# A decoder layer on one core: the sparse heads' scaling and biases moved to GpSimd, the compressed branch's output matmul split in two f32r parts

## What is computed

```python
kc = compress(k_cmp, ...); vc = compress(v_cmp, ...)      # 31 compressed keys and values of each group
pc = softmax(q . kc - m * dist)                           # compressed branch
o_c = pc @ vc
ps = softmax(q . ks - m * dist)                           # selected blocks (at 512 tokens: all, causal)
pw = softmax(q . kw - m * dist)                           # sliding window of 512
o = gate0 * o_c + gate1 * (ps @ vs) + gate2 * (pw @ vw)
```

## Time and profile before

| | us |
|---|---|
| median of 3 runs | 859.66 (858.51 to 860.06) |
| the profiled execution | 861.95 |
| its span in the profile | 860.2 |
| TensorE busy | 826.0 (96%) |
| VectorE busy | 448.9 (52%) |
| ScalarE busy | 298.9 (35%) |
| GpSimd busy | 30.0 (3%) |
| mean granted TensorE clock, share of full speed | 0.991 |

### The profile page before, as it was taken

The page is one execution under the profiler, slowest core; times in us unless marked ns, Lnnn a source line. Parts: engine busy times, 40 slices in busy tenths (PEclk is TensorE's granted clock), DMA queues, the critical chain, the costliest instruction groups (busy, mean ns, idle before and its releaser), DMA issues.

```text
span 860.2 us, 10804 instructions
## 1 busy us (share of the span) xinstructions
PE 826.0 (96%) x4149; PEld 689.5 (80%) x4149; DVE 448.9 (52%) x868; ACT 298.9 (35%) x530; POOL 30.0 (3%) x35
## 2 busy tenths in 40 slices
PE   5999999999999899999999899999999999999993
PEld 4898899888887677778888688888888888888883
DVE  4733533554878888875653744433333334333336
ACT  6101145244255665654322622222222222322213
POOL 2300000000000000000310000000000000000003
PEclk9999999999999999999999899999999999999998
DMA  7931325231311011115433133333333332222202
GB/s 233 314 99 50 98 50 136 67 101 51 96 53 50 0 50 50 37 38 170 124 113 92 43 95 98 98 98 98 98 98 98 98 98 98 98 98 98 98 1 98
DMA packets 98501, 79.05 MB, mean 92 GB/s; under 512 B 16880, under 2 KB 92704, under 8 KB 98464
## 3 DMA queue, kind: packets, MB, share of 16 engines
q1 hardware_dynamic: 98368, 78.52, 30.5%
q10 hardware_dynamic: 96, 0.02, 0.0%
HBM read 75.34 MB, written 3.19 MB: 91 GB/s over the span
## 4 chain that ended last, share of the span: by engine, by line
PE 89%; DVE 5%; ACT 3%; issue 1%; DMA 1%; SPq 0%; ACTq 0%
PE bank L1265 26%; PE bank L1266 26%; PE bank L1267 26%; PE bank L1360 2%; PE bank L1330 2%; ACT probs L609 2%; PE bank L1476 2%; PE bank L1456 1%; PE bank L1441 1%; PE bank L1409 1%; DMA xs<-in_x_dram 1%; DVE probs L1087 1%; ACT probs_t_hi L687 1%; PE bank L1470 1%; PE bank L1285 1%
## 5 line engine op out<-in xcount | busy, mean ns | idle before, releaser
L1265 PE MATMUL bank<-h_hi,w_hi 128*128 128x512 f32 x352 | 138.7, 394 | 3.0 <-DVE h_lo L841 3.0
L1266 PE MATMUL bank<-h_lo,w_hi 128*128 128x512 f32 x352 | 138.0, 392 | 0.0
L1267 PE MATMUL bank<-h_hi,w_lo 128*128 128x512 f32 x352 | 137.9, 392 | 0.0
L1265 PE MATMUL bank<-n_hi,w_hi 128*128 128x512 f32 x288 | 115.0, 399 | 1.6 <-DVE gm L905 1.6
L1266 PE MATMUL bank<-n_lo,w_hi 128*128 128x512 f32 x288 | 112.4, 390 | 0.0
L1267 PE MATMUL bank<-n_hi,w_lo 128*128 128x512 f32 x288 | 112.4, 390 | 0.0
L786 DVE TENSOR_TENSOR w_lo<-w_raw,w_hi 128x2048 fp32r<-128x2048 f32 (+2 forms) x30 | 67.2, 2240 | 61.0 <-ACT w_hi L551 60.7
L551 ACT CAST w_hi<-w_raw 128x2048 fp32r<-128x2048 f32 (+2 forms) x30 | 55.6, 1855 | 73.1 <-PE bank L1267 62.2
L1265 PEld LDWEIGHTS bank<-h_hi,w_hi 128*128 128x128 f32 x352 | 66.7, 190 | 17.5 <-issue 3.5
L733 ACT ACTIVATE tanh_g<-gate_scaled 128x512 f32<-128x512 f32 x22 | 13.9, 632 | 187.1 <-DVE gate_scaled L1208 187.1
L1266 PEld LDWEIGHTS bank<-h_lo,w_hi 128*128 128x128 f32 x352 | 66.8, 190 | 14.1 <-issue 0.2
(11 more groups left out here) (200 smaller groups left out, 1264.5 us busy)
## 6 DMA issues: line engine op xcount, KB each, us to landing
w_raw<-in_w_ffn_in_dram SPq DMA_DIRECT2D x44, 512.0 KB, 4.7
w_raw<-in_w_in_dram SPq DMA_DIRECT2D x39, 512.0 KB, 4.8
w_raw<-in_w_ffn_out_dram SPq DMA_DIRECT2D x22, 512.0 KB, 3.6
w_raw<-in_w_out_dram SPq DMA_DIRECT2D x8, 512.0 KB, 4.1
xs<-in_x_dram SPq DMA_DIRECT2D x4, 512.0 KB, 6.8
wck_k<-in_w_ck_dram SPq DMA_DIRECT2D x1, 2048.0 KB, 10.7
wck_v<-in_w_cv_dram SPq DMA_DIRECT2D x1, 2048.0 KB, 17.3
w_raw<-in_w_in_dram SPq DMA_DIRECT2D x8, 256.0 KB, 4.5
```

What stands on the lines that cost most here:

```text
L1265: pe.matmul(dst, w[0], x_[0], start=start, stop=False)
L1266: pe.matmul(dst, w[0], x_[1], start=False, stop=False)
L1267: return pe.matmul(dst, w[1], x_[0], start=False, stop=stop)
```

## The change

The four scaling instructions of each of the 16 passes go from VectorE to GpSimd; VectorE keeps the reciprocal and the product with the gate (`pass_weights`). The biases of all 8 heads go to GpSimd, as two instructions each. The compressed branch's output matmul is made of f32r parts: the probabilities split into `pchi` (ScalarE) and `pclo` (VectorE), the values laid out per head of the group as [low | high] in 128 rows of which 32 are not zero (`vcst`, by GpSimd, once for each group). `vst` loses its block of zeros, and both `pthi` and `ptlo` meet [low | high]. Addresses in SBUF are shuffled to fit. The diff, without those and without the semaphores' declarations:

```diff
+            def stack_vc(g):
+
+                for r in range(4):
+                    rows = slice(CMP * r, CMP * r + CMP)
+                    ins = pool.tensor_copy(vcst[rows, r, HD:2 * HD], vc[rows, g, :])
+                ins.then_inc(vc_hi, 1)
+                pool.wait_ge(vc_hi, g + 1)
+                for r in range(4):
+                    rows = slice(CMP * r, CMP * r + CMP)
+                    ins = pool.tensor_tensor(vcst[rows, r, 0:HD], vc[rows, g, :],
+                                             vcst[rows, r, HD:2 * HD].bitcast(F32), ALU.subtract)
+                ins.then_inc(vc_ready, 1)
+
+            pool.wait_ge(cbias_ready, 1)
+            pool.wait_ge(kv_evac, 2)
+            pool.memset(vcst[:].bitcast(F32), 0.0).then_inc(vc_zeroed, 1)
+            pool.wait_ge(vc_zeroed, 1)
+            stack_vc(0)
+            pool.wait_ge(vc_ready, 1)
+
+            def nsa_bias(h):
+
+                if h >= 2:
+                    pool.wait_ge(s_max, 2 * h - 2)
+                pool.tensor_scalar(nbias[:, h % 2, :], dist[:], -SLOPE_NSA[h], 1.0, ALU.mult, ALU.mult).then_inc(nbias_part, 1)
+                pool.wait_ge(nbias_part, h + 1)
+                pool.tensor_tensor(nbias[:, h % 2, :], nbias[:, h % 2, :], cmask[:], ALU.add).then_inc(nbias_ready, 1)
+
+            def scale(n):
+
+                pool.wait_ge(pw_ready, n + 1)
+                for i in range(TT):
+                    q = sp[n % 2][:, Q_OFF[i]:Q_OFF[i] + P * (i + 1)]
+                    ins = pool.tensor_scalar(q, q, ust[:, n % 2, 3, i:i + 1], 1.0, ALU.mult, ALU.mult)
+                ins.then_inc(p_ready, 1)
+
+            nsa_bias(0)
+            nsa_bias(1)
+            for n in range(2 * NH):
+                scale(n)
+                if n == 8:
+                    pool.wait_ge(p_ready, n + 1)
+                    pool.wait_ge(o_ready, 7)
+                    stack_vc(1)
+                    pool.wait_ge(vc_ready, 2)
+                if n % 2 and n < 2 * NH - 4:
+                    nsa_bias(n // 2 + 2)
...
-                        act.copy(pc_t[:, g, :], ps[g][:]).then_inc(ct_evac, 1)
+                        act.copy(pchi[g][:], ps[g][:]).then_inc(pc_hi_ready, 1)
...
-                link(dve.memset(vc[:], 0.0))
...
-                dve.tensor_scalar(vc[:, :, 0:HD], ps[2][:, 128:256].rearrange("p (g d) -> p g d", g=2), 0.5, None, ALU.mult).then_inc(kv_evac, 1)
+                dve.tensor_scalar(vc[:], ps[2][:, 128:256].rearrange("p (g d) -> p g d", g=2), 0.5, None, ALU.mult).then_inc(kv_evac, 1)
                 cmp_bias()
-                nsa_bias(0)
-                nsa_bias(1)
...
+            def cmp_turn():
+                for g in range(2):
+                    dve.wait_ge(pc_hi_ready, g + 1)
+                    dve.tensor_tensor(pclo[g][:], ps[g][:], pchi[g][:].bitcast(F32), ALU.subtract).then_inc(pc_lo_ready, 1)
...
-                if m < 2:
-                    dve.tensor_tensor(v[:, :, 2 * HD:], ident[:, 0:HD].unsqueeze(1).to_broadcast([P, TT, HD]),
-                                      ident[:, 0:HD].unsqueeze(1).to_broadcast([P, TT, HD]), ALU.subtract)
...
+                if n % 2 == 0:
+                    dve.wait_ge(nbias_ready, n // 2 + 1)
...
-            def scale(n):
+            def pass_weights(n):
...
+                if n >= 2:
+                    dve.wait_ge(p_ready, n - 1)
                 link(dve.reciprocal(ust[:, n % 2, 2, :], ust[:, n % 2, 1, :]))
-                link(dve.tensor_tensor(ust[:, n % 2, 3, :], ust[:, n % 2, 2, :], gate[:, :, 3 * h + 1 + b], ALU.mult))
-                for i in range(TT):
-                    q = sp[n % 2][:, Q_OFF[i]:Q_OFF[i] + P * (i + 1)]
-                    ins = dve.tensor_scalar(q, q, ust[:, n % 2, 3, i:i + 1], None, ALU.mult)
-                ins.then_inc(p_ready, 1)
+                dve.tensor_tensor(ust[:, n % 2, 3, :], ust[:, n % 2, 2, :], gate[:, :, 3 * h + 1 + b],
+                                  ALU.mult).then_inc(pw_ready, 1)
...
-                    elif n < 12:
-                        nsa_bias(n // 2 + 2)
...
-                    pe.wait_ge(ct_evac, 2)
+                    pe.wait_ge(pc_lo_ready, 2)
...
-                    pe.matmul(o[:], vc[CMP * j:CMP * j + CMP, g, :], pc_t[CMP * j:CMP * j + CMP, g, :],
-                              start=True, stop=False)
+                    pe.wait_ge(vc_ready, g + 1)
+                    for p_ in (pchi[g], pclo[g]):
+                        pe.matmul(o[:], vcst[:, j, :], p_[:], start=(p_ is pchi[g]), stop=False)
...
-                    for c, p_ in ((0, pthi), (HD, ptlo)):
-                        ins = pe.matmul(o[:, P * k:], vst[b][:, k, c:c + P], p_[:, K_OFF[k]:K_OFF[k] + P * (TT - k)],
-                                        start=False, stop=(b == 1 and k == TT - 1 and c == HD))
+                    for p_ in (pthi, ptlo):
+                        ins = pe.matmul(o[:, P * k:], vst[b][:, k, :], p_[:, K_OFF[k]:K_OFF[k] + P * (TT - k)],
+                                        start=False, stop=(b == 1 and k == TT - 1 and p_ is ptlo))
```

More of the change, by code:

```diff
@@ L229, in trunk @@
         kst = at("k_stack", [2, 2, S], E + 15360, F32R)
-        vst = [at(f"v_stack{b}", [TT, 192], o, F32R)
-               for b, o in enumerate((Dd + 32768, G + 11264))]
+        vst = [at(f"v_stack{b}", [TT, 2 * HD], Dd + 32768 + 2048 * b, F32R) for b in range(2)]
         ytmp = at("y_tmp", [S], E + 6144)
@@ L244, in trunk @@
         maskc = at("maskc", [TT, CMP], G + 6656)
-        pc_t = at("pc_t", [2, S], G + 7168)
+        pchi = [at(f"pc_hi{g}", [S], G + 7168 + 2048 * g, F32R) for g in range(2)]
+        pclo = [at(f"pc_lo{g}", [S], G + 11264 + 2048 * g, F32R) for g in range(2)]
         hs = at("hs", [4, 2 * CMP], G + 11264)
         kc = at("kc", [2 * CMP], G + 12288)
-        vc = at("vc", [2, 2 * HD], G + 4608)
+        vc = at("vc", [2, HD], G + 4608)
+        vcst = at("vc_stack", [4, 2 * HD], G + 5120, F32R)
         w2k = at("w2k", [2, 2, HD], G + 13056)
@@ L251, in trunk @@
         crows = at("crows", [P], G + 14592)
[L252 to L256, removed]
+        cst = at("cst", [2, 32], G + 15104)
+        cvec = at("cvec", [48], G + 15360)
+        gate = at("gate", [TT, NH * 3], G + 15552)
+        st = at("st", [4, 8], G + 15936)
+        ust = at("ust", [2, 4, TT], G + 16064)
         dm = at("dm", [NG, TT, 4], G + 16192)
@@ L315, in trunk @@
             sem(k) for k in ("dp_ready", "dt_ready", "dt_evac_act", "dt_evac_dve", "do_ready", "do_evac"))
-        cs_ready, cs_added, cs_sub, cs_exp, cp_ready, ct_ready, ct_evac = (
-            sem(k) for k in ("cs_ready", "cs_added", "cs_sub", "cs_exp", "cp_ready", "ct_ready", "ct_evac"))
+        cs_ready, cs_added, cs_sub, cs_exp, cp_ready, ct_ready, pc_hi_ready, pc_lo_ready = (
+            sem(k) for k in ("cs_ready", "cs_added", "cs_sub", "cs_exp", "cp_ready", "ct_ready",
+                             "pc_hi_ready", "pc_lo_ready"))
+        pw_ready, nbias_part, nbias_ready = (sem(k) for k in ("pw_ready", "nbias_part", "nbias_ready"))
+        cbias_ready, vc_zeroed, vc_hi, vc_ready = (sem(k) for k in ("cbias_ready", "vc_zeroed", "vc_hi", "vc_ready"))
         gate_tanh, gate_ready = sem("gate_tanh"), sem("gate_ready")
@@ L865, in cmp_bias @@
                                                    in1=maskc[:], op0=ALU.mult, op1=ALU.add)
[L866 to L870, removed]
+                ins.then_inc(cbias_ready, 1)
             def tile(n):
@@ L1015, in cmp_scores @@
                 dve.wait_ge(cs_ready, 1)
+                dve.wait_ge(cbias_ready, 1)
                 for i in range(TT):
@@ L1123, in _ @@
                     cmp_scale()
+                elif job == "cmp_turn":
+                    cmp_turn()
                 elif job == "cmp_scores":
@@ L1128, in _ @@
                     if n == 0:
-                        scale(0)
+                        pass_weights(0)
                 elif job == "turn":
@@ L1132, in _ @@
                     if n < 15:
-                        scale(n + 1)
+                        pass_weights(n + 1)
                     else:
```

## The result

| | before | after |
|---|---|---|
| median of 4 runs each, same chip (us) | 859.15 (858.51 to 860.06) | 865.75 (865.64 to 867.56) |
| the profiled execution | 861.95 | 867.56 |
| its span | 860.2 | 865.5 |
| mean granted TensorE clock | 0.991 | 0.985 |

The ratio of the times is 1.0071, with an interval of 1.0052 to 1.0091: slower by 0.7%, some 6 us. The forecast for the median was 861.8 with slower as the likeliest sign, so the sign and the range hold, and the size is short by some 4 us. One execution among all that follow, experiment 3's first with 1204.65 us and a granted clock of 0.65, was disturbed and enters no ratio.

The account below looks back on a forecast made before the run. TensorE bounds steps with a tile, a ring of ScalarE, VectorE and TensorE the others. Terms -4.0 + 0.3 + 3.8 + 1.7 + 0.8 + 0.6 - 1.1 = +2.1 us, from 859.66 to 861.8 us; range 857 to 872.

Parts of the forecast that it names:

- The saving is not there: Rival: the new 128-row f32r pair costs what the old 32-row pair did; 865.8 us, chance 0.03.
- Compressed matmul, -4.0: Compressed branch's output matmul on TensorE: the f32r pair shortens a step to 2.95 us, saving 0.8 at five places.
- Its price before the stage, +0.3: VectorE's two added subtractions before the stage delay L988, so TensorE's transposes wait some 0.3 us.
- Scaling, five laps at 0.78, +3.8: Steps without a tile: GpSimd's pass of 1.85 us for VectorE's 1.27, plus a 0.2 hop, lengthens five laps.
- VectorE's operations in the way, +1.7: VectorE's split_q and split_v slip between GpSimd's scaling instructions, making turn(4) later by 0.69 us and turn(8) by 1.04.
- The rival that no stopping takes place: GpSimd's one-input instructions run beside VectorE's or come first; 858.4 us, 857.5 or less with a faster pass; chance 0.27.
- Step 0, +0.8: Stage's first step: turn(0) starts 1.7 us later, while a tile's 0.9 us wait for an eviction goes.
- w_lo against GpSimd, +0.6: VectorE's w_lo waits up to a microsecond on GpSimd's scaling or a bias, and the next tile's eviction behind it.
- VectorE's relief, -1.1: Without scaling VectorE is no longer late for the minima of pass 5, so the 1.2 us wait on L1074 goes.
- The scaling on GpSimd: Step pricing a GpSimd pass at 1.85 us from the affine select; each bare lap 0.78 longer, five laps +3.8 us.
- two-input price: Rival: a GpSimd scaling pass costs 3 us or more, the ring bounds nearly every step; 880 us, chance 0.13.
- it did not even out: Denies the rival that VectorE's relief gives a microsecond or two more than counted; 860 us, chance 0.09.

Follow-up runs that it names:

- experiment 3: Kernel before with only the scaling of the probabilities moved to GpSimd, biases left on VectorE; 868.70 us, ratio 1.0096; second series 870.51 us, 1.0117.
- Experiment 2: Kernel before with only the compressed branch's output matmul changed to f32r parts, scaling and biases still on VectorE; 857.22 us, ratio 0.9959.
- experiment 6: Kernel after, but VectorE's low part of the next head's queries waits until the pass before it is scaled; 867.64 us, ratio 1.0073.
- Experiment 8: Kernel after, but in passes 0, 3, 4, 5, 8, 11 VectorE scales the 384 and 512 column pieces, GpSimd the other two; 856.97 us, ratio 0.9956.
- experiment 1: Kernel after with matmuls nobody reads put on TensorE before its waits for scaled passes 0, 3, 4, 5, 8, 11; 861.89 us, ratio 1.0016 to before.
- after's repeat: Kernel after, unaltered, timed once more in a later series; 865.94 us, ratio 1.0057 to before.
- Experiment 5: Kernel before with three more VectorE multiplies by 1.0 of 512 columns in passes 3, 4, 5, 8 and 11; 871.65 us, ratio 1.0120.
- experiment 7: Kernel after with GpSimd's scaling written as one operation, without the second multiply by 1.0; 890.48 us from one execution.

## Why the prediction was right in sign and short in size

The sign was right, and the terms that are in the sum come out near their size (below, some 1.5 us for 2.1). The range held with some luck: it was drawn wide for the price of a pass on GpSimd, and what took the time from 861.8 to 865.75 was the clock, which no term and no rival has. It is chance, too, that the rival *The saving is not there* names 865.8: the saving is there.

- **Compressed matmul, -4.0.** Right. The chain of after has, in the step of the earlier trace rows's kind, these pieces (start us, us, what):

```profile
267.09 1.27 PE bank L1490 x8
268.37 0.46 PE bank L1521 x2
268.83 1.22 PE bank L1526 x8
```

  That is 2.95 us, the forecast's figure to the last digit. It was gained at five turns (1, 7, 9, 13, 15) and lost in a wait at the others. Experiment 2 has 3.5 of the expected 3.7.
- **Its price before the stage, +0.3.** 0.46: the first scores start at 250.70, in before at 250.24. VectorE's two subtractions end at 238.31 (238.1 in the forecast), and TensorE then waited 0.23 and 0.33, so the wait came twice, not once.
- **Scaling, five laps at 0.78, +3.8.** The price of a pass was 2.05, not 1.85, and the extra hop not 0.2 but about 0.1: 283.71 to 283.80 from VectorE to GpSimd, 285.85 to 285.91 on to TensorE, against the 0.06 of before. The two errors have opposite signs: 0.88 a lap by the parts and 0.8 at turns 3 and 11 in the table. The wait for the scaling was forecast at some 12 us in 6 or 7 waits and was 13.9 in 6; turns 6, 12 and 14 had none.
  The Trainium skill (GPSIMD Engine Reference, section 4.1) says that a one-input operation is roughly at line rate on GpSimd. The estimate from it was 1.1 us a pass. The trace has 2.05, and the measurement decides: the better guide was the affine select of the earlier trace rows, with 1.85.
- **VectorE's operations in the way, +1.7.** Pass 4 was stretched by 0.51 (2.56 against 2.05, confirmed by experiment 6) where 0.69 was forecast, and pass 8 by 0.60 (2.65) where 1.04 was, though q_stack and v_stack both fell into it; VectorE's v_stack had its share, with 0.59 us for the 0.43 it takes alone. 1.1 in all. The rival that no stopping takes place has fallen.
  The Trainium skill (SBUF — State Buffer, section on who interferes with whom) gives it as a rule that a VectorE instruction with two SBUF inputs locks out a GpSimd instruction that reads SBUF. The trace agrees, here for a GpSimd instruction with one tensor input; the stretch was 0.51 us for a q_stack of 0.69. Experiment 8 shows that VectorE's one-input scaling holds GpSimd up as well: the pieces of 128 and 256 columns took 1.21 us beside it (1.21 to 1.23 in all six shared passes), and 0.37 + 0.48 = 0.85 in the undisturbed pass 3 of after, whose four pieces the groups of 283.7 to 285.9 us show apart (the next number behind the busy time is the mean ns):

```profile
L569 POOL TENSOR_SCALAR probs<-probs,ust 128x512 f32<-128x512 f32 x1 | 0.7, 692 | 0.0
L569 POOL TENSOR_SCALAR probs<-probs,ust 128x384 f32<-128x384 f32 x1 | 0.6, 585 | 0.0
L569 POOL TENSOR_SCALAR probs<-probs,ust 128x256 f32<-128x256 f32 x1 | 0.5, 478 | 0.0
L569 POOL TENSOR_SCALAR probs<-probs,ust 128x128 f32<-128x128 f32 x1 | 0.4, 371 | 6.6 <-DVE ust L1136 6.6
```
- **Step 0, +0.8.** Turn(0) came 2.0 later (1.7 forecast, and the stage itself began 0.46 later), the eviction wait of 0.9 went, and the scores behind the tile came 0.89 later, half of it brought along: +0.4.
- **w_lo against GpSimd, +0.6.** Not there. GpSimd's biases were stretched by it (1.1 us on the mean, with two of 2.53; 0.62 otherwise), but nothing waited for them; the one eviction wait left is 0.8, for 0.7 before.
- **VectorE's relief, -1.1.** -0.9: turn(5) comes no later than turn(4) though its pass is 0.9 longer, and the wait for the minima of pass 5 is gone. With five laps at 0.8 the terms so measured make -4.0 + 0.5 + 4.0 + 1.1 + 0.4 - 0.9 = 1.1, with 0.88 a lap 1.5; the table leaves 1.6.
- **The step that failed** is "The scaling on GpSimd", in "Each bare lap is longer by 1.85 - 1.27 + 0.2 = 0.78 [...] Five laps: +3.8". It priced a longer wait at its own length and took for granted that TensorE works behind it as before. Its waits before the change were 0.8, 1.4, 1.5 and 0.7 us long, and the clock stayed at 1.00. Made 2.2 to 2.8 long, three of them were followed by some microseconds at the 1.2 GHz level. The table gives that 4.9 us and experiment 1 gives it 4.7 (3.5 by after's repeat). Experiment 5 shows the same with GpSimd idle. It even shows in the sign that the prediction had for the lap of step 3, near 6.8 us: from cast to cast it took 7.3 (279.78 to 287.08), with transposes of 2.37 in it. With the waits filled the run stands at 861.89, 1.4 us over before by its ratio, where the sum had 2.1. Why just these three waits were followed by a fall stays open.

The other rivals: no two-input price (2.05, not 3 or more), and it did not even out (relief 0.9 where 1.1 was counted).

## What to carry to other kernels

Before making a wait of TensorE longer in a ring of engines, look at the granted clock of the stretch and of others behind long waits: a wait of 1.5 to 3 us cost its own time here and in many cases the slower matmuls behind it, most where a tile stands there (2.6 us at turn 9). If the wait can't be had shorter, matmuls that nobody reads gave the clock back here (45 of them, 3.5 to 4.7 us of 866). Move work to a slower engine only in steps where a bound engine hides it, and then ask whether it brings anything at all: here the part that was hidden brought nothing, and the scaling as a whole (experiment 3) cost 8 to 10 us where its terms in the sum, 3.8 + 1.7 + 0.8 + 0.6 - 1.1, had 5.8.

## What the runs showed of the hardware that was not expected

- The granted clock fell behind waits of TensorE of 1.5 to 2.9 us (0.50 to 0.77 from 286 to 292 us, behind turn(3), in after, its repeat and experiments 3 and 5). The length of the single wait does not decide it: turn(8) waited 2.84 us in after and 2.83 in its repeat, with a fall in the first alone; turn(11) of experiment 3 and turn(3) of experiment 4 waited 1.51 each, again with a fall in the first alone. The Trainium skill (TensorE: Matmul & The Clock Gate, section on HAM oscillation) describes a pattern like it: bursts of matmuls between waits, each burst starting at the lower clock. Its example waits for DMA, and every burst starts low; here waits for GpSimd or VectorE did it, and three of the five long waits in after's laps were followed by a fall.
- GpSimd's multiply by a value of each partition is up to twice as fast with a second, idle operation as with one: 2.05 against 4.26 us for the undisturbed pass 3 (after and experiment 7), 878 against 1646 ns on the mean for 512 columns, 476 against 708 for 128. Why is not settled; no experiment asks for the cause.
- GpSimd's distance times slope from int32 took 0.62 us for 512 columns in six of eight cases and 2.53 in the other two, under a w_lo of VectorE, as in the earlier trace rows.
